# Attention scores of two head groups issued together, an even and an odd head in turn, into two PSUM banks

## The reference

```python
scores = jnp.einsum('bnqhgd,bnjhd->bnhgqj', qb, kb).astype(jnp.float32) * (HEAD_DIM ** -0.5)
scores = jnp.where(valid[None, :, None, None], scores, NEG_INF)
probs = jax.nn.softmax(jnp.concatenate([scores, sink], axis=-1), axis=-1)[..., :-1]
out = jnp.einsum('bnhgqj,bnjhd->bnqhgd', probs.astype(vb.dtype), vb)
```

## Time and profile before

| | |
|---|---|
| median of 3 runs | 1633.47 us (1630.47 to 1635.81) |
| the profiled execution | 1636.02 us, its span 1634.2 us |
| PE busy | 1583.0 us, 97% of the span |
| DVE, ACT busy | 1148.0 us (70%), 902.9 us (55%) |
| mixer attention, layer 0 and 1 | steps 0 to 11 from 161.9 to 217.6 us, and 721.8 to 777.5 us |
| second block's attention | steps 0 to 15 from 1195.4 to 1267.4 us |

### The profile page before, as it was taken

How to read it: one execution, slowest core, us unless ns; L and a number is a source line. 1 busy time by engine, 2 the same in 40 slices (tenths; PEclk the granted TensorE clock), 3 DMA queues, 4 the chain that set the end, 5 groups by cost and what they waited for, 6 DMA issues and landing times.

```text
span 1634.2 us, 20218 instructions
## 1 busy us (share of the span) xinstructions
PE 1583.0 (97%) x8036; PEld 1300.7 (80%) x8036; DVE 1148.0 (70%) x1615; ACT 902.9 (55%) x1377; POOL 80.2 (5%) x75
## 2 busy tenths in 40 slices
PE   7999999999999999999999999999999869999997
PEld 7988887786888799888877678888757758888785
DVE  7457756657455583677567588856665679999998
ACT  5467544435344354765435355444353558888885
POOL 0010000001000000100000000000200000000005
PEclk9999999999999999999999999999999979999999
DMA  7535336436555354543446288764431319999994
GB/s 281 194 148 198 119 105 222 171 122 257 208 189 196 129 211 176 206 165 120 145 164 232 98 336 315 296 240 157 163 140 42 118 69 345 367 371 376 369 379 167
DMA packets 52200, 339.34 MB, mean 208 GB/s; under 512 B 7835, under 2 KB 8477, under 8 KB 13316
## 3 DMA queue, kind: packets, MB, share of 16 engines
q1 hardware_dynamic: 48932, 331.79, 55.1%
q0 software_dynamic: 3168, 6.20, 1.0%
HBM read 332.82 MB, written 10.49 MB: 210 GB/s over the span
## 4 chain that ended last, share of the span: by engine, by line
PE 83%; DVE 10%; ACT 3%; DMA 2%; issue 1%; POOL 1%; SPq 0%; DVEq 0%; ACTq 0%
PE bank L735 23%; PE bank L737 23%; PE bank L736 22%; PE bank L741 4%; DVE wls L2064 4%; PE bank L803 2%; PE bank L869 2%; PE bank L967 2%; DMA raw<-in_ws_dram 2%; DVE h L2034 1%; ACT whs L1457 1%; PE bank L986 1%; POOL sm L3000 1%; PE bank L1222 1%; PE bank L1240 1%
## 5 line engine op out<-in xcount | busy, mean ns | idle before, releaser
L2064 DVE TENSOR_TENSOR wls<-raw,whs 128x1024 fp32r<-128x1024 f32 x442 | 524.9, 1227 | 200.6 <-ACT whs L1457 199.7
L1457 ACT ACTIVATE whs<-raw 128x1024 fp32r<-128x1024 f32 x442 | 445.0, 1052 | 239.4 <-PE bank L737 168.3
L735 PE MATMUL bank<-whs,P1h 128*128 128x512 f32 (+1 forms) x732 | 290.6, 397 | 3.8 <-issue 2.3
L737 PE MATMUL bank<-whs,P1l 128*128 128x512 f32 (+1 forms) x732 | 285.1, 390 | 0.0
L736 PE MATMUL bank<-wls,P1h 128*128 128x512 f32 (+1 forms) x732 | 284.6, 389 | 0.0
L735 PE MATMUL bank<-whs,P0h 128*128 128x512 f32 (+1 forms) x640 | 256.7, 401 | 2.5 <-DVE P0l L2034 1.2
L737 PE MATMUL bank<-whs,P0l 128*128 128x512 f32 (+1 forms) x640 | 249.5, 390 | 0.0
L736 PE MATMUL bank<-wls,P0h 128*128 128x512 f32 (+1 forms) x640 | 249.5, 390 | 0.0
L735 PEld LDWEIGHTS bank<-whs,P1h 128*128 128x128 f32 x732 | 138.1, 189 | 32.9 <-issue 4.6
L737 PEld LDWEIGHTS bank<-whs,P1l 128*128 128x128 f32 x732 | 137.9, 188 | 29.0
L736 PEld LDWEIGHTS bank<-wls,P1h 128*128 128x128 f32 x732 | 138.1, 189 | 26.7
(11 more groups left out here) (276 smaller groups left out, 2485.4 us busy)
## 6 DMA issues: line engine op xcount, KB each, us to landing
raw<-in_ws_dram SPq DMA_DIRECT2D x264, 1024.0 KB, 4.8
landing<-in_ws_dram SPq DMA_DIRECT2D x38, 1024.0 KB, 7.0
lnb<-in_ln_g_dram SPq DMA_DIRECT2D x6, 512.0 KB, 5.7
lnb<-in_ln_b_dram SPq DMA_DIRECT2D x6, 512.0 KB, 6.5
ydram<-arena POOLq DMA_DIRECT2D x4, 512.0 KB, 11.9
mid<-in_bias_dram SPq DMA_DIRECT2D x1, 2048.0 KB, 8.1
h<-in_x_dram SPq DMA_DIRECT2D x2, 512.0 KB, 4.3
lnb<-in_mem_dram SPq DMA_DIRECT2D x1, 1024.0 KB, 13.0
```

The costliest lines, as they stand in the source:

```text
L735: e.matmul(out, x[0], w[0], start=start, stop=False, skip_group_check=skip)
L737: return e.matmul(out, x[1], w[0], start=False, stop=stop, skip_group_check=skip)
L1457: e.activation(hi, src, ACT.Copy, bias=0.0, scale=1.0).then_inc(*high.done(n, f))
L2064: e.tensor_tensor(lo, src, f32(hi), ALU.subtract).then_inc(*low.done(n, f))
```

## The change

The scores of an even group and of the following odd group are now issued in one step, the even step. The matmuls alternate: an even head into bank 4, then an odd head into bank 5. The two banks are both waited for ahead of the first matmul. The odd step issues no scores. The other engines' programs are as before, instruction for instruction; each group still has its own signal.

```diff
                 def scores(i):
                     t, h0, nh = groups[i]
-                    w, b = 128 * (t + 1), 4 + i % 2
+                    w = 128 * (t + 1)
                     pe.wait_ge(act, "qT", l, 1, 1)
                     pe.wait_ge(vec, "kT", l)
-                    bank(b, (vec, "sc", l, i))
+                    for o in range(2):
+                        bank(4 + o, (vec, "sc", l, i + o))
                     for j in range(nh):
-                        hd = h0 + 2 * j
-                        p = 64 * (hd % 2)
-                        m = e.matmul(banks[b][:, j * w:(j + 1) * w], qT[p:p + 64, hd // 2, t * 128:(t + 1) * 128],
-                                     kT[p:p + 64, hd // 8, 0:w], start=True, stop=True)
-                    m.then_inc(*mm.done("sc", l, i))
+                        for o in range(2):
+                            hd, p = h0 + o + 2 * j, 64 * o
+                            m = e.matmul(banks[4 + o][:, j * w:(j + 1) * w], qT[p:p + 64, hd // 2, t * 128:(t + 1) * 128],
+                                         kT[p:p + 64, hd // 8, 0:w], start=True, stop=True)
+                            if j == nh - 1:
+                                m.then_inc(*mm.done("sc", l, i + o))
...
-                    if i < n:
+                    if i < n and i % 2 == 0:
                         scores(i)
```

More of the change, by code:

```diff
@@ L1218, in scores2 @@
                 t, hd = items[i]
-                b, p = 4 + i % 2, 64 * (hd % 2)
                 pe.wait_ge(vec, "qk", 5)
-                bank(b, (vec, "sc2", i))
-                e.matmul(banks[b][:, :], q2T[p:p + 64, hd // 2, t * 128:(t + 1) * 128], k2T[p:p + 64, hd // 2, :],
-                         start=True, stop=True).then_inc(*mm.done("sc2", i))
+                for o in range(2):
+                    bank(4 + o, (vec, "sc2", i + o))
+                for o in range(2):
+                    p = 64 * o
+                    e.matmul(banks[4 + o][:, :], q2T[p:p + 64, hd // 2, t * 128:(t + 1) * 128], k2T[p:p + 64, hd // 2, :],
+                             start=True, stop=True).then_inc(*mm.done("sc2", i + o))
             def turn2(i):
```

## The result

The changed kernel takes 1614.38 us (median of 4 runs, 1612.66 to 1615.64) against 1632.41 us for the kernel before (4 runs): a ratio of 0.9883, 95% interval 0.9866 to 0.9900. It is 18 to 19 us faster. The direction, the overlap of the two halves and the bank wait came as forecast. The size did not, because of a limit on the overlap that is not there.

The account below looks back on a forecast made before the run. PE time was taken as the bound; two mixers at -3.3 us each and the second block at -3.9 sum to -10.5 us, giving 1623.0 us. The range ran from 1618.2 us to 1 us above Rival 1's 1631.1.

Parts of the forecast that it names:

- What bounds the kernel: Whole kernel: PE time counts, busy 97% of the span; in mixer attention each PE microsecond saved comes off the end.
- What a group costs: Score groups in mixers and second block: 1.27 us of PE each, 0.40 of it for switching to 64 rows and back.
- The second term: Score pairs: odd streams partly overlap even ones; tile-1 pair saves 1.06 us, item pair 0.85, 128-column overlap nothing.
- the case that every odd stream is free: Mixer tile-1 pairs: with all odd streams overlapped, another 0.2 us saved per pair.
- The third term: Step 2 of each mixer: PE waits about 1.7 us for bank 5, starts 1.3 us late; 0.9 behind at step 4.
- The second block's first six items: Items 0 to 5: new waits offset the pairs' savings; net 0 us, between -0.5 and +1.5.
- items 6 to 13: Second block, steps 6 to 13: four pairs save 0.85 us each, 3.4 us in all.
- the last pair: End of the second block: worth about 0.5 us, as the chain from there runs over DVE and ACT.
- Rival 1: All pairs: no overlap, only ways in and out saved; -2.4 us, 1631.1 us; chance 22%.
- Rival 2: Mixers: 128-column weight loads overlap as well; -4.7 us per mixer, -13.3 in all, 1620.2 us; chance 15%.
- Rival 3: All pairs: each change between array halves costs 0.2 us; +12 us, 1645.5 us; chance 8%.
- Rival 4: Longer PE waits at step 2 lower the clock: 1626.4 us if once, 1629.8 if in both mixers; chance 5%.

Follow-up runs that it names:

- same_half: Changed kernel with both groups of a pair reading partitions 0 to 63: 1634.46 us, ratio 1.0019 to the kernel before.
- experiment 2: Changed kernel with all even-group matmuls of a mixer pair ahead of all odd ones, second block unchanged: 1616.35 us, ratio 0.9899.
- second_only: Changed kernel with the mixers' scores put back as before, so only the second block is paired: 1626.47 us, ratio 0.9970.
- mixers_only: Changed kernel with the second block's scores put back as before, so only the two mixers are paired: 1620.7 us, ratio 0.9922.
- experiment 5: Changed kernel with second-block items 0 to 5 issued singly and only items 6 to 15 in pairs: 1622.02 us, ratio 0.9923.
- experiment 4: Changed kernel with one of its two score functions put back: mixers_only 1620.7 us, second_only 1626.47 us.
- experiment 1: The same_half run: changed kernel with both groups of a pair on partitions 0 to 63, 1634.46 us, ratio 1.0019.
- changed_again: Changed kernel, no further edit, measured again on the same chip as second_late: 1614.58 us, ratio 0.9877.
- changed_third: Another profile of the changed kernel, no further edit: 368.5 us from item 14 to the end; no whole time given under this name.
- second_late: The run of experiment 5: changed kernel with second-block items 0 to 5 unpaired, 1622.02 us, ratio 0.9923.

## Why the prediction was wrong

**What bounds the kernel** held in the main. Between the two traces PE is busy for 28.3 us less and the span is 22.5 us shorter; PE idles for the other 5.8 us, most of it in new waits. In the runs it is 18 to 19 us.

**What a group costs** held: 1.27 us, of it 0.40 for the ways in and out. same_half gave 2.13 us for a pair on one half, where I had 2.12.

**The second term failed**, at the sentence that "even at best only the second instruction of one head lies beside the first of the next", and at "for 128 columns I expect nothing". Both come from one assumption, that matmuls and loads of the two halves take turns in program order. They don't: with four even instructions ahead in the program the odd half still ran beside the first (experiment 2), and loads run in twos. So a tile-1 pair costs 1.28 us and not 1.48, an item pair 1.27 and not 1.69, a tile-0 pair 1.28 and not 2.16. Four tile-0, eight tile-1 and eight item pairs make 4 x 0.88 + 8 x 0.2 + 8 x 0.42 = 8.5 us, if none is lost in waits. The forecast missed the runs by 7.5 to 9. By stage, at the same clock: a mixer gained 5.4 us (step 0 of mixer 0 to step 0 of mixer 1 is 558.2 us in second_only and 552.8 in mixers_only, neither with a low clock there) where I had 3.3, and items 0 to 5 gained 2.3 where I had 0. I had read the pace of 0.11 us as one of weight loads in general; between the halves it does not hold. I had named the case that every odd stream is free (another 0.2 us a tile-1 pair) but gave it no rival, so the range began above the measured time.

The rule of the Trainium skill that I cited (TensorE: Matmul & The Clock Gate, Part 3) had the overlap, and the trace agrees: starts 7 ns apart. The limit of order I had put on top. The same part says that matmuls keep program order in their starts; here experiment 2 disagrees, with two of opposite halves running at 177.68 us while the program has four of one half first. The measurement decides.

**The third term**, the wait for bank 5 at step 2, was right in place and cause, and the chain after shows each link that was named. I had 1.7 us of idle PE and 1.3 us of lateness; it is 1.97 us idle, and step 2 starts 8.79 us behind step 0 instead of 8.07, 0.7 us late. The shorter pair makes PE arrive earlier, so it waits longer and ends less late. same_half has pairs of the length that I had assumed and shows the term as I worked it out: step 2 starts 9.46 us behind step 0 (I had 171.3 - 161.9 = 9.4), after a wait of 1.74 us. With the short pairs the term changes its sign: from step 0 to step 4 it is 16.5 us in mixers_only, without a low clock, against 17.0 before, which is the 0.5 us early that I had put down for overlapping loads.

**The second block's first six items** I had put at 0 (-0.5 to +1.5). They gain 3.9 us in the trace, 2.3 at the same clock (experiment 5). The waits that I feared are there (2.07 us at step 2, 0.98 at step 4) and eat the gain of the first two pairs: item 4 starts 19.1 us behind item 0, 1.7 of it lost to the clock, against 17.6 before. The gain comes between steps 4 and 6, where item 5's matmul is gone (1.27 us) and PE's wait of 1.72 us has shrunk to 0.69. In items 6 to 13 it is the reverse: four pairs save 4 x 1.27 = 5.1 us of PE, and 3.0 arrive where I had 3.4, since PE now waits 1.7 us there, 0.99 of it ahead of item 14's pair. What the last pair brings, against my 0.5, is not shown (experiment 4).

**The rivals.** Rival 1, no overlap, is experiment 1, and its number was too kind by 3 to 4 us: pairing alone is worth nothing. Rival 2 came closest, yet still had the limit of order in it; without it (8 x 0.2 and 8 x 0.42 us less) it would have had 1615.2 by count. Rival 3, a price for changing halves, is out: with 26 such changes in each mixer a pair takes as long as one group did. Rival 4, the clock, came in layer 0's mixer (0.80 over 8.7 us, 1.7 us lost) and not in layer 1's; in two further profiles of the same kernel it came in both.

What stays open: how far ahead PE looks for the other half's instruction in general (with four of one half's instructions ahead it starts at once, with eight it starts late), whether the clock falls behind the wait by chance, and what shortened the last stretch.

## What to carry to other kernels

Matmuls over 64 rows that sit in opposite halves of the partitions, write different banks and stand near each other in the program cost in fp32 as much as one of them, loads included (whether the banks must differ was not tested); put such pairs side by side, in turn, and look first for work that already has both halves. Then ask who frees the second bank: scoring a group a step earlier takes a step of slack from its reader, and in the mixers the slack was less than a step at just one place, step 2; in the second block PE waits at several steps. When such a wait shows, shorten the chain that ends in it (the copy ahead of the exponentials, in ACT's idle time, brought 4 us); moving its work behind the wait moved the wait and made it longer.

## What was not expected of the hardware

- Weight loads of the two halves run in twos: 16 loads and 16 matmuls of 128 columns in 1.16 us from the first start to the last end, against 2.05 us when all use one half. In the score groups of before no two loads start closer than 0.11 us; in the changed kernel those of the two halves start 7 ns apart.
- The halves are not served in strict program order. With 4 instructions of one half ahead the other starts 14 ns behind the first; with 8 ahead it starts beside the fifth, and the whole takes 1.71 us.
- A wait of PE of 1.97 us was followed by the lower clock in layer 0's mixer and not in layer 1's (the same wait, in the same trace). In changed_again, changed_third and second_late it was followed by it in both mixers, in mixers_only in neither: seven falls in ten such waits. Whether a wait costs the clock as well is thus not settled by its length alone.
